# A two-block transformer kernel on one core: its beginning loaded in other pieces and another order

## The reference, cut to what matters

```
u  = rmsnorm(x) * norm_mix                 # 256 x 1024
p  = u @ w_in                              # parts: gq, gk (256 columns each), gv (512), dq, dk, dv, ...
z  = gr @ gate_w + gate_b                  # gr: 16 columns of p; gates of the linear attention
```

## Time and profile before

| | |
|---|---|
| median of 3 runs (lowest, highest) | 1003.78 us (1003.42, 1004.11) |
| the profiled execution: time | 1003.68 us |
| its span | 1001.7 us |
| TensorE busy | 845.3 us (84%) |
| VectorE, ScalarE busy | 463.9 us (46%), 331.0 us (33%) |
| mean granted clock of TensorE | 0.928 of full |

### The profile page before, as it was taken

One profiled execution on the slowest core, in us unless ns is written; L12 is line 12 of the kernel. 1 busy time (PEld: TensorE's weight loads), 2 busy tenths in 40 slices (PEclk: granted clock), 3 DMA queues, 4 the chain that ended last, 5 costly groups with the idle time before them and its releaser, 6 DMA issues.

```text
span 1001.7 us, 13218 instructions
## 1 busy us (share of the span) xinstructions
PE 845.3 (84%) x5361; PEld 587.3 (59%) x5361; DVE 463.9 (46%) x912; ACT 331.0 (33%) x553; POOL 23.3 (2%) x35
## 2 busy tenths in 40 slices
PE   8999999999995665848466576758999999999997
PEld 8787888898741131313122131312887899999995
DVE  5788766574611030302103021102867788565695
ACT  5666744754210000100000010001444655545532
POOL 1021010100000000000000000000000000000000
PEclk9999999999997887877878877987999999999999
DMA  8753466597999999999999999999555444353531
GB/s 306 274 168 126 166 225 231 192 385 268 355 426 436 432 426 433 432 428 432 432 430 431 432 428 429 425 436 387 196 173 177 136 148 167 129 168 129 206 128 43
DMA packets 57580, 294.73 MB, mean 294 GB/s; under 512 B 3922, under 2 KB 4532, under 8 KB 49204
## 3 DMA queue, kind: packets, MB, share of 16 engines
q1 hardware_dynamic: 56068, 290.84, 73.8%
q10 hardware_dynamic: 1456, 3.10, 0.8%
HBM read 292.88 MB, written 1.05 MB: 293 GB/s over the span
## 4 chain that ended last, share of the span: by engine, by line
PE 55%; DMA 34%; DVE 5%; ACT 3%; issue 2%; SPq 1%; POOL 0%; POOLq 0%; ACTq 0%; DVEq 0%
PE bank L2533 12%; PE bank L2535 11%; PE bank L2534 11%; DMA uT<-in_down_units 10%; DMA uT<-in_gate_units 9%; DMA ring<-in_down_units 6%; DMA uT<-in_up_units 6%; PE bank L2953 4%; PE bank L2976 3%; PE bank L2467 2%; DVE ring_rounded L1480 2%; DMA ring<-in_first_blocks 2%; ACT ring_rounded L946 2%; PE bank L2927 1%; PE bank L3065 1%
## 5 line engine op out<-in xcount | busy, mean ns | idle before, releaser
L1480 DVE TENSOR_TENSOR ring_rounded<-ring,ring_rounded 128x2048 fp32r<-128x2048 f32 x76 | 174.2, 2292 | 110.7 <-ACT ring_rounded L946 110.4
L946 ACT ACTIVATE ring_rounded<-ring 128x2048 fp32r<-128x2048 f32 x75 | 143.6, 1914 | 160.5 <-PE bank L2535 151.4
L2953 PE MATMUL bank<-ring,main 128*32 128x512 f32 x768 | 106.9, 707 | 59.1 <-DMA ring<-in_up_units 55.1
L2534 PE MATMUL bank<-ring_rounded 128*128 128x256 f32 (+1 forms) x456 | 143.8, 315 | 0.0
L2535 PE MATMUL bank<-ring_rounded 128*128 128x512 f32 x320 | 125.0, 391 | 0.0
L2953 PEld LDWEIGHTS bank<-ring,main 128*32 128x32 f32 x768 | 26.9, 127 | 132.3 <-issue 88.0
L2533 PE MATMUL bank<-uT_rounded,ring_rounded 128*128 128x256 f32 x320 | 92.8, 290 | 0.0
L2535 PE MATMUL bank<-uT_rounded,ring_rounded 128*128 128x256 f32 x320 | 90.7, 283 | 0.0
L2534 PEld LDWEIGHTS bank<-ring_rounded 128*128 128x128 f32 x456 | 87.0, 191 | 5.0
L2533 PE MATMUL bank<-ring_rounded,uT_rounded 128*128 128x512 f32 x208 | 83.1, 400 | 1.6 <-ACT main L1308 0.8
L2976 PE MATMUL bank<-ring,main 128*32 128x512 f32 x352 | 56.2, 797 | 32.5 <-DMA ring<-in_down_units 32.5
(11 more groups left out here) (353 smaller groups left out, 1376.3 us busy)
## 6 DMA issues: line engine op xcount, KB each, us to landing
ring<-in_up_units SPq DMA_DIRECT2D x11, 4096.0 KB, 33.4
ring<-in_w_in SPq DMA_DIRECT2D x42, 1024.0 KB, 5.0
ring<-in_gate_units SPq DMA_DIRECT2D x10, 4096.0 KB, 33.3
ring<-in_down_units SPq DMA_DIRECT2D x10, 4096.0 KB, 31.7
main<-in_gate_units SPq DMA_DIRECT2D x4, 3072.0 KB, 30.4
main<-in_down_units SPq DMA_DIRECT2D x3, 3072.0 KB, 32.7
main<-in_up_units SPq DMA_DIRECT2D x3, 3072.0 KB, 30.2
ring<-in_w_ckv SPq DMA_DIRECT2D x8, 1024.0 KB, 5.1
```

The lines of the kernel that those rows point to most:

```text
L946: a.activation(rounded(hi_half(name, h)), raw_half(name, h), ACT.Copy).then_inc(hi_made, 1)
L1480: v.tensor_tensor(rounded(raw), raw, as_f32(hi_half(name, h)), ALU.subtract).then_inc(split_made, 1)
L2534: mm(dst, left[0], right[1], start=False, stop=False, skip_group_check=True)
L2953: last = mm(bank[2 + part][on, :], xg3[:, h * (KC // 2) + k, on], weight_unit(unit_buffer(j, p, u), e, KC)[:, k, :], start=h + k == 0, sto ...
```

## The change

The scales and biases are turned on the host: `gain_columns` returns the transposed array, and one transfer brings it to `cols` directly. The tile `rows`, its transpose, the PSUM use `cols` and ScalarE's copy go; `None` keeps its place in `PSUM_PLAN`, and `USE` counts without it, so all other uses keep their banks. Engines that waited for `cols` to be drained wait for the transfer.

`xT` is loaded in four parts of 256 KB, one before each quarter of weights, instead of in two of 512 KB. The first quarter of weights comes as two chunks of 256 KB. ScalarE follows this order: one piece of `x`, then its quarter of weights; the first quarter is copied in two instructions of 512 columns. VectorE's order stays as it was (`split_first` waits for counts one higher). TensorE makes the first hi x hi products chunk by chunk (4 and 4), and 6 constant products in place of 14.

```diff
-PSUM_PLAN = ["cols"]
+PSUM_PLAN = [None]
...
-USE = {name: (n % 8, n // 8) for n, name in enumerate(PSUM_PLAN)}
+USE = {name: (n % 8, sum(other is not None for other in PSUM_PLAN[n % 8:n:8]))
+       for n, name in enumerate(PSUM_PLAN) if name}
...
-            sp.dma_start(rows[0:N_COLS, :], A["rows"]).then_inc(rows_landed, 16)
+            sp.dma_start(cols[:, :], A["columns"]).then_inc(cols_landed, 16)
             for j in range(2):
-                at = slice(j * 1024, (j + 1) * 1024)
-                sp.dma_start(lo_a[:, at], A["xT"][:, at]).then_inc(xT_landed[j], 16)
                 for q in range(2):
+                    at = slice((2 * j + q) * 512, (2 * j + q + 1) * 512)
+                    sp.dma_start(lo_a[:, at], A["xT"][:, at]).then_inc(xT_landed[2 * j + q], 16)
                     landed = (first_landed[j], raw_landed[j])[q]
                     part = 4 * j + 2 * q
-                    sp.dma_start(quarter(raw_half("gqk", j), q).rearrange("p (k n) -> p k n", k=2),
-                                 SOURCE["gqk"][:, part:part + 2, :]).then_inc(landed, 16)
+                    dst = quarter(raw_half("gqk", j), q).rearrange("p (k n) -> p k n", k=2)
+                    for lo, n in ((0, 1), (1, 1)) if part == 0 else ((0, 2),):
+                        sp.dma_start(dst[:, lo:lo + n, :], SOURCE["gqk"][:, part + lo:part + lo + n, :])\
+                            .then_inc(first_chunk_landed if part + lo == 0 and n == 1 else landed, 16)
...
-            copy("cols", cols[:, :], N_COLS)
-            wait_drained(act, "cols")
+            act.wait_ge(cols_landed, 16)
             for j in range(2):
-                act.wait_ge(xT_landed[j], 16)
-                raw_hi("x", uT_flat, lo_a, "norm_mix", (2 * j, 2 * j + 1))
                 for q in range(2):
-                    act.wait_ge((first_landed[j], raw_landed[j])[q], 16)
-                    a.activation(rounded(quarter(hi_half("gqk", j), q)), quarter(raw_half("gqk", j), q), ACT.Copy)\
-                        .then_inc(first_hi, 1)
+                    act.wait_ge(xT_landed[2 * j + q], 16)
+                    raw_hi("x", uT_flat, lo_a, "norm_mix", (2 * j + q,))
+                    hi, raw = quarter(hi_half("gqk", j), q), quarter(raw_half("gqk", j), q)
+                    for n, at in enumerate((slice(0, 512), slice(512, 1024)) if j + q == 0 else (slice(0, 1024),)):
+                        landed = first_chunk_landed if j + q + n == 0 else (first_landed[j], raw_landed[j])[q]
+                        act.wait_ge(landed, 16)
+                        a.activation(rounded(hi[:, at]), raw[:, at], ACT.Copy).then_inc(first_hi, 1)
...
-                    dve.wait_ge(first_hi, 2 * h + q + 1)
+                    dve.wait_ge(first_hi, 2 * h + q + 2)
...
             keep_busy(wait_free("xrow0"), 5)
-            pe.wait_ge(rows_landed, 16)
-            b = wait_free("cols")
-            full("cols", transpose(b[:, 0:N_COLS], rows[0:N_COLS, :]))
-            keep_busy(wait_free("xrow0"), 14)
+            pe.wait_ge(cols_landed, 16)
+            keep_busy(wait_free("xrow0"), 6)
...
-                for x_part, w_part, chunks in ((0, 0, (0, 1)), (0, 0, (2, 3)), (1, 0, range(4)), (0, 1, range(4))):
+                first_chunks = ((0,), (1,), (2, 3)) if h_ == 0 else ((0, 1), (2, 3))
+                for x_part, w_part, chunks in [(0, 0, c) for c in first_chunks] + [(1, 0, range(4)), (0, 1, range(4))]:
...
-                        pe.wait_ge(first_hi, 2 * h_ + q + 1)
+                        pe.wait_ge(first_hi, 1 if chunks == (0,) else 2 * h_ + q + 2)
```

More of the change, by code:

```diff
@@ L262, in build @@
         rope = sb("rope", [P, TT, 2 * HD])
-        rows = sb("rows", [P, P])
         cols = sb("cols", [P, N_COLS])
@@ L416, in build @@
         mem_landed, mem2_landed = sem("mem_landed"), sem("mem2_landed")
-        xT_landed = [sem(f"x_channels_landed{j}") for j in range(2)]
+        xT_landed = [sem(f"x_channels_landed{j}") for j in range(4)]
+        first_chunk_landed = sem("first_block_first_chunk_landed")
         memT_landed, mem2T_landed = sem("mem_channels_landed"), sem("mem2_channels_landed")
         inputs_split, rows_spread = sem("input_channels_split"), sem("row_factors_spread")
-        rows_landed, params_landed = sem("rows_landed"), sem("params_landed")
+        cols_landed, params_landed = sem("columns_landed"), sem("params_landed")
         gates_landed, lambdas_landed = sem("gates_landed"), sem("lambdas_landed")
@@ L1501, in _ @@
             link(v.memset(chunk_start[:, :].rearrange("p (c t) -> p c t", t=GLA_CHUNK)[:, :, 0:1], 0.0))
-            wait_drained(dve, "cols")
+            dve.wait_ge(cols_landed, 16)
             def raw_lo(prefix, raw, hi, gain, chunks=range(4)):
@@ L3272, in rope_table, with gain_columns @@
     return np.concatenate([cos, cos, -sin, sin], axis=1).astype(np.float32)
-def gain_rows(inputs):
+def gain_columns(inputs):
     rows = []
@@ L3281, in gain_rows @@
         rows.append(np.concatenate([vector] * (n * P // vector.size)).reshape(n, P))
-    return np.concatenate(rows)
+    return np.concatenate(rows).T
 def in_partitions(w):
@@ L3341 @@
             "down_units": lambda: down_in_units(inputs["w_e_down"]),
-            "rope": rope_table, "rows": lambda: gain_rows(inputs), "router": lambda: router_rows(inputs),
+            "rope": rope_table, "columns": lambda: gain_columns(inputs), "router": lambda: router_rows(inputs),
             "router_b": lambda: router_bias(inputs), "w_gr": lambda: low_rank_rows(inputs),
```

## The result

The changed kernel takes **1004.74 us** (median of 20 runs, 1003.76 to 1005.93), the kernel before 1003.50 (20 runs beside them, 1002.67 to 1004.37). The ratio is 1.0014, with 95% from 1.0008 to 1.0020: a loss of about 0.14%, small but outside the uncertainty. The times of the changed kernel lie in two groups, eleven from 1003.76 to 1004.82 and nine from 1005.38 to 1005.93. The profiled execution took 1005.66 us and is one of the upper group, so its trace shows more than the mean loss.

A forecast was written before the change was run, and what follows sets the result against it. Two paths meet at 32.39 us: VectorE's sets it, TensorE's is 0.2 shorter. TensorE's +0.15 fits the slack, so 1003.68 + 0.1 + 0 = 1003.78, less a tenth for landings: 1003.7 us; own range 1003.3 to 1004.1, wide 1002.8 to 1005.4.

The forecast's parts named there:

- A: Rival: clock falls between the two early product bursts, three us at half speed; +1.1, 1004.8 us; chance 0.16.
- C: Rival: long stall before the low-rank products, x's last quarter late; 1004.3 to 1005.1 us; chance 0.14.
- The second gap: TensorE, after the first eight products: a wait of 1.2 to 2 us ending near 11, behind the second quarter's copy.
- the text's worst case: Last part of x lands only with the fourth quarter at 15.63: w_gr ready at 17.85, 1.55 us late.
- 0.15 after TensorE wants it: VectorE's w_gr before the low-rank products: ready at 16.45 with landings 0.3 earlier; +0.15 on TensorE's path.
- they are no work on either path; they only keep TensorE awake: Constant products at TensorE's beginning, cut from 14 to 6: no work on either path, nothing in the sum.
- B: Rival: the same clock fall lasting six us, no gain in landings; +2.4, 1006.2 us; chance 0.09.
- the slack of 0.2: At 32.39, TensorE's path is 0.2 us shorter than VectorE's; a loss on it counts only above that.
- the landings: Weights' transfers land between 0.9 us earlier and 0.25 later; -0.3 taken, a tenth in the final sum.
- D: Rival: everything, gv too, lands 0.9 us earlier through the scales' transfer alone; 1003.2 us; chance 0.11.
- two engines then hold back the weights behind them: Scales' 82-row transfer: its two engines stay behind for every later landing; the sum would take -0.9 for weights.

The follow-up runs named there:

- with 14 products: Changed kernel with 14 constant products in place of 6: 1003.93 us, second sample 1004.34, mean 1004.20 ± 0.16.
- the gap filled: Changed kernel with 7 more constant products between the first hi x hi products and the wait for the second quarter: 1004.72 us.
- the order alone: Kernel before with only x in four parts, one ahead of each quarter of weights: 1004.58 us, ratio 1.0013.
- early masks: Kernel before with the four masks built and cast before x's row mean: 1003.06 us; with columns too, 1002.74 and 1003.15.
- the kernel before with 6: Kernel before with 6 constant products in place of 14: 1004.08 us, ratio 1.0006.
- the changed one with 10: Changed kernel with 10 constant products in place of 6: 1004.61 us, ratio 1.0012.
- the columns alone: Kernel before with cols loaded directly, no transpose or copy: 1003.88 us, ratio 1.0004.
- the two with `x` before the third quarter: Two samples of the changed kernel with 14 constant products and x's last two parts both before the third quarter of weights: 1004.19 and 1003.66 us.
- the delayed kernel: Kernel before with 9 constant products put in front of gv's first product: 1005.12 us, ratio 1.0013.
- 20 products: Changed kernel with 20 constant products in place of 6: 1004.09 us, ratio 1.0006.
- the version without constant products: Changed kernel with 0 constant products behind the wait for the scales, where it had 6: 1004.96 us, ratio 1.0014.

## Why the forecast of no change was wrong

The forecast was 1003.7 us, no change. It came out slower, by 1.24 (medians of 1004.74 and 1003.50): inside the wide range of 1002.8 to 1005.4 but outside the forecast's own, 1003.3 to 1004.1, and slower by a clear margin with this many runs. Rivals A (1004.8) and C (1004.3 to 1005.1) named the two mechanisms that the traces show. That each also has the size is luck: A reached it with a fall of 3 us and 0.2 of slack, C by a stall alone, and on the mean each part makes about half of the loss.

**Right.** The second quarter of weights is copied at 10.05 for 10.24, so the first products (7.74, forecast 8.15) gain nothing but these 0.2 us at 11.25. The second gap is there, 1.83 us within the forecast 1.2 to 2. `w_gr` is late for the reason given: with 14 products, the gap filled or the order alone it holds TensorE for 0.56 to 0.66 us, and the low-rank products start at 16.57 to 16.77 where 16.0 to 16.6 was forecast. The text's own terms give such a stall: with all landings 0.3 earlier TensorE wants `w_gr` at 16.0 and has it at 16.45, and the "0.15 after TensorE wants it" is the shift against the kernel before, not the wait. In the first profile `w_gr` is ready at 17.90, as in the text's worst case (17.85). A shift behind 50 us is carried: the way from VectorE's subtraction near 53 us to the issue near 280 is 226.2 to 226.4 us in every trace.

**Wrong: "they are no work on either path; they only keep TensorE awake".** That is the step that failed. The cost of removing eight of them was put at nothing and the fall treated as a rival with 0.25 of the chance, since the new beginning was as like the one as like the other stretch of the earlier trace rows. But the nearest rows held less for the good case than I read in them. The one that stayed up had 1.46 of 3.3 us in one pattern of gaps; here 1.97 of 3.40 and 1.56 of 3.30 did not stay up. A busy share from another stage does not decide it. Size: in the profile the 40 products take 7.44 us and with early masks 5.02 (5.02 or 5.03 in four more traces without a fall), 2.4 more, near B's 2.6 for a fall of six us. B carried all but 0.2 of that to the end; in fact `w_gr` would have held TensorE anyway, and 0.5 us (first profile) to 1.2 (second) of it delayed what follows, with 0.5 to 0.7 over all executions. That the two groups of times are executions with and without a fall is not shown. Both profiles of the changed kernel are of the upper group (1005.66 and 1006.03), but the profiled executions with a fall of the kernel before with 6 and of the changed one with 10 took 1004.08 and 1004.66, and with 14 products, where no profile has a fall, single executions took up to 1005.58.

**Wrong: the slack of 0.2.** The sum took it off every loss on TensorE's path. It was read as the length of one wait in one execution, and both matter. The wait at 32.39 is 0.18 us long, but from `gv`'s first product to the copy near 43 TensorE needs 0.6 us more with it than without it (17.3 and 16.7 us in the table). And it is not the same in each execution: 0.8 by the same reading with the columns alone, 1.0 in the two with `x` before the third quarter; the delayed kernel gives 0.6 on the mean. So the stall of 0.6 us ought to vanish in the slack in such executions, and in the profiled ones it does. The means say that the changed order with 14 products is 0.55 ± 0.17 slower all the same. It may come from executions in which the weights land early. There the old order can start `gv` at 25.7, as the delayed one would have, and its VectorE is early too, while the new order is held by `w_gr`: it starts `gv` at 26.72 to 26.91 with the stall, 26.49 with 20 products, although `gv` had landed by 20.5 to 21.5. This is argued: no undisturbed execution of the old order with an early landing and the clock up was profiled.

**Wrong: the landings.** I took -0.3 of the bounds -0.9 to +0.25. Columns alone gave 1003.90 ± 0.17 against 1003.65: there is no gain to be found, and D is out. The Trainium skill ("DMA: Bandwidth & Descriptors", on why a DMA increments its semaphore by 16) gives 2 engines for 82 rows; no view here shows whether it was so. That two engines then hold back the weights behind them was the text's own inference, and it is not borne out: a hold-up of 0.9 us that ended should have shown in the time, and the second quarter lands within the same bounds with rows and with columns.

**On direction.** The Trainium skill's warning that short bursts with waits between them close the clock gate again ("TensorE: Matmul & The Clock Gate", HAM oscillation) was cited and given too little weight. The four traces with 6 or 10 constant products and unfilled gaps agree with it.

**Left open.** What the 0.55 of the changed order is made of: the stall is in the traces but costs nothing in them up to 280 us, and the profiled executions with 14 products took 1003.38 and 1003.83, less than their mean of 1004.20, so the slower ones have no trace. The first quarter in two chunks was not tried alone, nor were 2 KB rows without the order. Open too are why the filled gap is still 0.8 above the kernel before on the mean, why the third quarter landed so late in the changed kernel's first profile, and the scatter of the order alone.

## What to carry to other kernels

Products that compute nothing may be load-bearing: before removing some, look at the granted clock over the gaps that they fill, and count the products behind the next gap at half speed, up to where another input would have made TensorE wait anyway. Work brought forward is worth only what the next input allows: here two microseconds of earlier products were given back at once, and left a wider gap. And the length of a wait read in one profile is not the slack of the path: compare whole stretches with and without the wait, in more than one execution. What helped here was to look at what stands on the slower path and could be done at another time, as the four casts.

## What was not expected of the hardware

- The same transfers land 0.8 to 1.6 us apart in different executions. The second quarter's copy starts at 10.24 in the kernel before and at 9.44 and 9.47 in two others with the same transfers, the third's at 14.29, 12.66 and 12.77, `gv`'s at 21.76, 20.55 and 20.78.
- The clock column reads 1.00 before the first rise though products run at half rate: 19 products in 4.08 us and, right behind, 23 in 2.60 (rows of the version without constant products).
- After a fall the clock is at 0.50 for 3.3 to 6.8 us with TensorE busy for most or all of it (5.45 of 6.80 us in the changed kernel, 3.40 of 3.40 with 10 products): full work does not bring it back at once.
- A wait of 0.18 us at 32.39 goes with 0.6 us more between `gv`'s first product and the copy near 43, one of 0.41 with 0.8, one of 0.60 with 1.0.
- Behind 280 us, in the stage of the experts above all, the versions' traces differ by -0.2 to +1.3 us from the kernel before's on their own, which hides effects of this size in a single comparison.
